# Attention scores as products over all 128 rows, with queries spread into zero-padded tiles by GpSimd

## The reference, cut to what matters

```python
HEAD_DIM = 64; N_HEADS = 8; QB = 128          # Lp = 640 positions, 16 of them meta tokens

def _diff_attention(q, k, v, lam, cid):        # q, k: (B, Lp, H, 2, 64); v: (B, Lp, H, 128)
    qf = q.astype(jnp.float32) * (HEAD_DIM ** -0.5)
    def block(i):                              # 128 queries at a time
        ...
        s = jnp.einsum('bqhmd,bkhmd->bhmqk', qb, kf)
        mask = cid[None, :] <= qc[:, None]     # block-causal, chunks of 64 positions
        p = jax.nn.softmax(jnp.where(mask, s, NEG_INF), axis=-1)
        a = p[:, :, 0] - lam * p[:, :, 1]
        return jnp.einsum('bhqk,bkhe->bqhe', a, vf)
```

## Time and profile before

| | |
|---|---|
| median of 3 runs | 1799.08 us (1799.01 to 1804.68) |
| profiled execution, its own time | 1799.66 us |
| its span, first to last instruction | 1797.8 us |
| mean granted TensorE clock, share of full | 0.996 |
| TensorE busy | 1774.3 us (99%) |
| VectorE busy | 1408.3 us (78%) |
| ScalarE busy | 1000.7 us (56%) |
| GpSimd busy | 331.6 us (18%) |
| line 918 (scores), share of the chain that ended last | 1% |

### The profile page before, as it was taken

How to read it: one execution, slowest core, us unless ns; L and a number is a source line. 1 busy time by engine, 2 the same in 40 slices (tenths; PEclk the granted TensorE clock), 3 DMA queues, 4 the chain that set the end, 5 groups by cost and what they waited for, 6 DMA issues and landing times.

```text
span 1797.8 us, 31963 instructions
## 1 busy us (share of the span) xinstructions
PE 1774.3 (99%) x13102; PEld 1673.3 (93%) x13102; DVE 1408.3 (78%) x2496; ACT 1000.7 (56%) x1960; POOL 331.6 (18%) x220
## 2 busy tenths in 40 slices
PE   9899999999999999999999999999999999999998
PEld 8899999978899989999889999999898999999987
DVE  6998968678756789969878996889367898689844
ACT  7553332668734447546556665666346566566632
POOL 1786343200000012011002211220000122122000
PEclk9999999999999999999999999999999999999999
DMA  6685222201132158466346876784332677578531
GB/s 183 148 185 133 80 94 95 71 24 37 59 100 94 60 142 181 123 159 143 121 115 138 175 157 149 148 174 122 112 95 77 133 172 154 141 153 170 123 114 71
DMA packets 263520, 221.29 MB, mean 123 GB/s; under 512 B 7126, under 2 KB 255759, under 8 KB 263374
## 3 DMA queue, kind: packets, MB, share of 16 engines
q1 hardware_dynamic: 186270, 180.96, 32.6%
q0 software_dynamic: 77088, 38.28, 17.3%
q10 hardware_dynamic: 16, 0.00, 0.0%
HBM read 217.12 MB, written 2.10 MB: 122 GB/s over the span
## 4 chain that ended last, share of the span: by engine, by line
PE 90%; DVE 5%; ACT 4%; issue 1%; DMA 0%; SPq 0%; DVEq 0%; ACTq 0%
PE ps L730 38%; PE ps L689 35%; PE ps L1338 6%; PE ps L1387 5%; DVE wlo L2385 1%; PE ps L918 1%; PE ps L1176 1%; PE ps L1151 1%; ACT p L1660 1%; PE ps L1167 1%; PE ps L1179 1%; DVE ast L2709 1%; ACT whi L1421 1%; PE ps L943 0%; DVE p L2723 0%
## 5 line engine op out<-in xcount | busy, mean ns | idle before, releaser
L2385 DVE TENSOR_TENSOR wlo<-raw,whi 128x1024 fp32r<-128x1024 f32 (+1 forms) x321 | 390.8, 1223 | 158.5 <-ACT whi L1421 157.5
L1421 ACT ACTIVATE whi<-raw 128x1024 fp32r<-128x1024 f32 (+1 forms) x373 | 391.4, 1052 | 215.9 <-PE ps L689 63.7
L689 PE MATMUL ps<-nhi,whi 128*128 128x256 f32 (+3 forms) x1072 | 250.9, 292 | 2.2 <-DVE clo L2693 0.8
L730 PE MATMUL ps<-nhi,whi 128*128 128x256 f32 (+2 forms) x876 | 250.0, 285 | 0.1
L730 PE MATMUL ps<-nhi,wlo 128*128 128x256 f32 (+2 forms) x876 | 247.0, 282 | 0.0
L689 PE MATMUL ps<-nhi,wlo 128*128 128x256 f32 (+3 forms) x1072 | 246.8, 289 | 0.0
L730 PE MATMUL ps<-nlo,whi 128*128 128x256 f32 (+2 forms) x876 | 246.8, 282 | 0.0
L730 PE MATMUL ps<-thi,whi 128*128 128x256 f32 x784 | 225.2, 287 | 2.1 <-DVE wlo L2385 0.7
L730 PE MATMUL ps<-thi,wlo 128*128 128x256 f32 x784 | 221.6, 283 | 0.0
L730 PE MATMUL ps<-tlo,whi 128*128 128x256 f32 x784 | 221.4, 282 | 0.0
L689 PE MATMUL ps<-nlo,whi 128*128 128x256 f32 (+3 forms) x944 | 209.8, 288 | 0.0
(11 more groups left out here) (517 smaller groups left out, 4102.4 us busy)
## 6 DMA issues: line engine op xcount, KB each, us to landing
raw<-in_w_in_dram SPq DMA_DIRECT2D x90, 1024.0 KB, 5.8
raw<-in_w_up_dram SPq DMA_DIRECT2D x22, 1024.0 KB, 5.1
raw<-in_w_out_dram SPq DMA_DIRECT2D x20, 1024.0 KB, 4.8
s1t<-in_w_in_dram SPq DMA_DIRECT2D x59, 256.0 KB, 3.2
s1t<-in_w_in_dram POOLq DMA_DIRECT2D x59, 256.0 KB, 7.3
raw<-in_w_in_dram POOLq DMA_DIRECT2D x59, 256.0 KB, 4.6
raw<-in_w_down_dram SPq DMA_DIRECT2D x16, 512.0 KB, 3.5
raw<-in_w_conv_out_dram SPq DMA_DIRECT2D x4, 1024.0 KB, 4.8
```

Source lines behind the costliest of these rows:

```text
L689: mm = eng.matmul(o, w, m[:, k, a:b], start=begins, stop=final and n == len(ks) - 1 and i == 2)
L730: mm = eng.matmul(o, w[:, k, :], m[:, k, :], start=start and k + i == 0, stop=stop and k == 3 and i == 2, skip_group_check=True)
L1421: eng.activation(hi, raw, ACT.Copy).then_inc(*A.up("hi", s))
L2385: eng.tensor_tensor(lo, raw, hi.bitcast(F), ALU.subtract).then_inc(*V.up("lo", s))
```

## The change

Two tiles `QZ[0]` and `QZ[1]`, each with four slots of 128 columns, are cleared once by GpSimd. For every step GpSimd then copies rows 0 to 63 of the query block into a slot of `QZ[0]` and rows 64 to 127 into the same slot of `QZ[1]`; the other map's rows stay zero. The scores of map m become a product of `QZ[m]`'s slot with all 128 rows of the keys. The copies of the first four steps stand among the `low` pieces of the last projections; those of the other 28 steps come after the clearing of the `AT` tiles, and each of them waits until the scores four steps earlier have been made. Before it goes on, GpSimd waits for its own copies. TensorE waits for GpSimd's copies in place of the queries.

```diff
+        QZ = [at(f"qz{m}", [128, 4, 128], F, o_raw + 2 * 8192 + 4096 + 2048 * m) for m in range(2)]
...
                     for m in range(2):
-                        r = slice(64 * m, 64 * m + 64)
-                        on.wait_ge(A("q", h), *key_in(h), *free(*banks[m]))
-                        eng.matmul(sv[:, m, c0 + a:c0 + b], Q[r, h, 2 + 128 * t:130 + 128 * t], K[r, h, a:b], start=True, stop=True) \
+                        on.wait_ge(G("qz", i), *key_in(h), *free(*banks[m]))
+                        eng.matmul(sv[:, m, c0 + a:c0 + b], QZ[m][:, i % 4, :], K[:, h, a:b], start=True, stop=True) \
                             .then_inc(*T.up("scores", i, m, a))
...
+            def spread_queries(i):
+                h, t, nk = head(i)
+                for m in range(2):
+                    r = slice(64 * m, 64 * m + 64)
+                    on.wait_ge(G.now(), A("q", h), i >= 4 and T("scores", i - 4, m, 0 if ORDER[(i - 4) % 4] < 3 else NM))
+                    op = eng.tensor_copy(QZ[m][r, i % 4, :], Q[r, h, 2 + 128 * t:130 + 128 * t])
+                    if m:
+                        op.then_inc(*G.up("qz", i))
+                    else:
+                        op.then_inc(*G.up())
+                on.wait_ge(G("qz", i))
...
                     eng.memset(V_[:, 0, :], 0.0).then_inc(*G.up("meta"))
+                    for m in range(2):
+                        eng.memset(QZ[m], 0.0).then_inc(*G.up())
+                elif s == slots.index((IN_REST - 2, BY_COL[0], False)):
+                    for i in range(4):
+                        spread_queries(i)
                 low(s)
             for i in range(2):
                 on.wait_ge(T("gate", 15))
                 eng.memset(AT[i][:, 4, :], 0.0).then_inc(*G.up("at_rows", i))
+            for i in range(4, 32):
+                spread_queries(i)
```

## The result

Over 14 runs each the changed kernel has a median of 1808.41 us (1806.61 to 1816.63), the kernel before 1801.63 (1798.95 to 1807.03). The ratio of the two is 1.0043, with a 95% interval of 1.0032 to 1.0053: slower, by 5.8 to 9.5 us, 7.7 in the middle; the two medians are 6.8 apart. Forecast was +8.6 and 1808.0, counted from 1799.08; the kernel before came out 2.6 us above that over these 14 runs. The profiled execution of the changed kernel took 1810.06 us with a span of 1808.2, 10.4 more than the span of before.

A forecast was written before the change was run, and what follows sets the result against it. TensorE's order was taken to set the pace from the second head on. Longer score groups +9.7 us, vanished wait -0.7, opening head -0.4 gave +8.6, stated as 1808.0 us, range 1804.5 to 1814.

The forecast's parts named there:

- What bounds the kernel: Attention stage: from the second head on TensorE's order sets the pace, one head taking 14.64 us.
- rival (a): A loop through VectorE and ScalarE sets each head's length; only the wide group's growth counts, +3.8 us; chance 0.09.
- The groups: A head's four score groups on TensorE grow from 4.16 to 5.37 us, +1.21 a head, +9.7 for eight.
- Rival (c): Full-row score passes stream at 0.46 ns a column, making the change faster by 6.3 us, 1793.4; chance 0.03.
- No switch at full rows: TensorE's full-row passes follow conv passes without a switch; 64-row groups pay 0.29 us each, 9.3 us for 32.
- The overlap: The two maps' 64-row score passes run together on TensorE; putting them one behind the other costs 19.6 us.
- The wait for the exponentials gone: TensorE's 0.14 us wait ahead of the wide group disappears in settled heads, five times, -0.7 us.
- rival (b): GpSimd's copies hold up VectorE, six a head at 0.3 us each, +10.7 us on top, 1818.9; chance 0.10.
- The opening: Opening head, to about 362 us: TensorE idles anyway, so its three narrow groups cost nothing, -0.4 us.
- GpSimd's work: Memsets of about 0.5 us each and 64 copies of 0.3 us stay hidden behind GpSimd's idling and early issue.
- The semaphore's price: TensorE's new wait on GpSimd costs 0 to 0.06 us a step, at most 1.9 us in all; taken as 0.

The follow-up runs named there:

- full rows alone: Kernel before with both maps' scores multiplying all 128 rows of Q and K, no GpSimd copies: ratio 1.0057, median 1812.70 us.
- both maps on one half: Kernel before with both maps' scores made from rows 0 to 63, so 64-row products can't overlap: ratio 1.0105, median 1820.62 us.
- copies only: Kernel before plus GpSimd's copies and TensorE's wait on them, scores still 64-row products from Q: ratio 1.0013, median 1803.99 us.

## Why the prediction was right

The difference came out at 7.7 us (5.8 to 9.5; 6.8 between the medians) for 8.6. That the time itself, 1808.41 us, lies 0.4 from the 1808.0 is luck in part: the kernel before had risen by 2.6 us in these runs. Step by step:

- **What bounds the kernel.** Right for the changed kernel: but for 0.13 us a head the order on TensorE set the pace, and the steady stretch grew by the sum of the groups. In the kernel before it was closer than the prediction had it. There TensorE's order takes 14.44 us of a settled head's 14.64; the other 0.20 (0.14 ahead of the wide group, 0.06 behind the 144 columns) are waits for rival (a)'s loop. That lead of 0.20 is small against the 1.2 by which TensorE's order grew, so (a), which would count the wide group alone, +3.8 in all, falls: full rows alone give 7.66 in the steady stretch.
- **The groups.** Predicted 1.03, 1.45, 0.60 and 2.29 us with the time ahead, sum 5.37. Measured, each with the 0.11 to 0.12 in front: 0.92 + 0.11, 1.34 + 0.11, 0.49 + 0.12, 2.24 + 0.20 in the head shown; the wide one is 2.16 + 0.12 where nothing is waited for (full rows without copies), and the sum then 5.37. The 0.84 ns a column from the mean's products held up to 512 columns, and so did 0.113 us for a pass of 16. Rival (c), 0.46 ns a column, falls.
- **No switch at full rows, 0.29 us for one at 64 rows.** Right on both, shown by the run with both maps on one half. The overlap was worth 2.37 us a head and the four switches 1.15. The Trainium skill, "TensorEngine Tiling (Array Packing)", section Key Properties, says that changing the mode drains TensorE; the trace agrees, with 0.29 us for each excursion, but that cost did not decide.
- **The wait for the exponentials gone, -0.7 us.** Half wrong: this is the term that was mis-sized. It goes with full rows alone, where the copies are absent; in the change about 0.16 us of it stays in a settled head, half ahead of the wide group and half inside it (15.89 against the 15.7 predicted). Two prices meet there. The prediction gave VectorE a slack of 0.27 us a head and put the copies' cost either inside it or, as rival (b), at 0.3 us for each of six. Measured where TensorE's groups are as before: the copies delay the head by 0.14 us through VectorE and ScalarE, about 0.02 us for each of six. So (b)'s mechanism acts, at less than a tenth of its price. The step that failed is the other price, of TensorE's new wait, taken as 0: 0.09 us, ahead of the wide group. An estimate from the rows of the changed kernel shows that it matters: the exponentials end at 425.28, and the pass ahead, started at 425.22, takes 0.12, so TensorE is free at 425.34; with the 0.04 us of the kernel before no wait would be left. Of the 0.23 us in all, 0.13 a head are left in the changed kernel, 0.44 in the steady stretch. The split rests on these rows alone: no run has the wait without the copies, or the copies without the wait.
- **The opening.** +8.6 holds 7.24 for the steady stretch (six heads at 1.21, with one wide and one 144-column group, 0.80 - 0.12, less 0.7) and 1.4 for the opening. The first was 8.10. The second was +1.4 in the execution with the lower clock and -0.25 in the one without. That the clock there might change was not among the steps at all; a forecast of 8.6 lies between the two outcomes, 7.85 and 9.5, partly by luck.
- **GpSimd's work.** The memsets took 526 ns each for 0.5, the first eight copies 2.75 us for 2.4, both hidden as said. All 64 took 0.465 us on average instead of 0.3, inside the bounds (the longest 1.17); two a step are 0.93 of a step of 4 us, and TensorE never waited on them. The semaphore's price, taken as 0, was 0 ahead of the narrow groups of the run with copies only, and 0.09 ahead of the wide ones, as above. The 0.06 us from which the prediction took its upper bound is no such price: it is the wait for ScalarE behind the 144 columns.

## What to carry over

Before row-half products are merged into full-row ones, look whether they overlap (two records with one start): the switches that such products cost are easy to see, 0.29 us each, and what their overlap saves is hidden in the lengths of the groups, here twice that. An idle engine's work isn't free because the engine is idle: it can lengthen instructions of a neighbour, and what that costs is set by the slack ahead of the next wait. A wait added to an engine cost nothing here where the engine was behind with its own work, and 0.09 us where another wait came last. Before a reordering is priced by what it saves on one engine, follow each in-order program that it delays: the one tried here made TensorE wait 1.63 us a head on ScalarE's order.

## What had not been expected of the hardware

- The clock in the opening: granted in full in three of five executions with full-row scores and in none of four with overlapped ones, worth 1.65 us (28.72 against 27.07). The cause is open.
- The hand-over from ScalarE to TensorE: 0.04 us where the weight load itself waits for ScalarE, 0.14 to 0.15 where it waits for another engine as well and the wait for ScalarE is an instruction of its own (51 ns).
- VectorE and GpSimd lengthen each other's instructions, by little for each: a VectorE addition of 514 columns from 686 to 761 ns, a GpSimd copy of 64 x 128 from 0.29 us to 0.80, and 1.78 for two.
- In some executions of these kernels TensorE waits 2.6 to 3.5 us outside the attention, once at 838 us behind a late transfer and else near 108 us for ScalarE, where the mean granted clock from 105 to 115 us is then 0.66 to 0.83. A difference of 8 us in 1800 is therefore read in the stretch that the change touches, not in the spans.
